# All fp32r products stream their columns backwards, and the weight ring moves by 256 bytes

## The chip, the cores and the metric

The kernel runs on one core of one Trainium2 chip. The metric is the device time of one launch in microseconds (us). The tensor engine (TensorE, PE in the profile) multiplies; VectorE (DVE), ScalarE (ACT) and GpSimd (POOL) do the rest; SyncE (SP) issues most of the DMAs. SBUF is the on-chip memory that TensorE reads; PSUM is the one that it writes.

## The reference

One decoder layer on an input of 256 tokens by 4096 channels, all in float32. Reduced to what costs time:

```
xn = rmsnorm(x);  p = xn @ w_in                 # 4096 -> 5200 columns, and the gates' 4096 -> 256
o_a, o_b, o_c, o_d = four causal attentions(p)  # 4 to 6 heads of 128 each
m = sum over branches: sigmoid(z @ gate_up[i]) * (o_i @ w_branch[i])   # -> 4096
h = x + m @ w_out                               # 4096 -> 4096
hn = rmsnorm(h);  q = hn @ peer_wq              # 4096 -> 1024, top-k expert keys
act = gelu(hn @ peer_u.T)                       # 4096 -> 4096
out = h + (sparse weights * act) @ peer_v       # 4096 -> 4096
```

Nearly all of the work is in the dense products with w_in, gate_up, w_branch, w_out, peer_wq, peer_u and peer_v.

## The kernel before

**Split products.** Each float32 operand is split into a high part in the type fp32r and a low part (value minus high part), also in fp32r. One float32 product becomes three fp32r matmuls: high times high, high times low, low times high. The activations are the stationary operand, a tile of 128 by 128 (512 bytes in each partition), kept transposed in `xt_hi`/`xt_lo` and, by stage, `x2_*`, `x3_*`, `ot_*`, `zt_*`, `s_*`. The weights are the moving operand, 512 columns wide (2048 bytes in each partition). They come from HBM in chunks of 256 rows by 512 columns.

**The weight ring.** A chunk s passes through slot s % 4 of three buffers: `w_raw` (SP's DMA), `w_hi` (ACT, line 1199: a rounding copy), `w_lo` (DVE, line 1608: raw minus high). TensorE waits for `hi_ready`, issues the eight matmuls that need `w_hi`, waits for `lo_ready`, issues the four that need `w_lo`, and raises `chunk_used`, which frees the slot. The three buffers stand one behind the other from `RG0`; every slot is 4096 bytes.

**Twelve matmuls to a chunk.** `products` (lines 668 to 684) runs two halves of 128 rows (j) times two halves of the tokens (h), three times over, into two PSUM banks. Each matmul has a stationary tile of its own, so each record of a matmul has a record of a weight load (LDWEIGHTS, engine PEld) beside it. The first group of columns (`first_products`, line 686) is 336 wide, all the others 512. `branch_products` (line 712) is the same by token half. In the products with w_out and peer_v, `fast_products` (line 1052) uses sums of operands, `t_*` moving against `xt_*` and `s_*` stationary, to save some matmuls; `plain_products` and `last_products` (line 1112, 256 columns wide) are the rest.

**Other users of TensorE.** Between chunks `between(s)` inserts the small work at fixed slots: transposes (line 780), attention scores and values in plain float32 (lines 854, 889 and others), one-hot products in bf16 (line 966). These are not fp32r.

**Where the tiles stand.** SBUF is laid out by hand: `XT0` is the base, `RG0` the ring 64 KB further, `MG0` a work area behind the ring, `CN0` constants behind that, and `PJ0` the projections behind the constants, where `x2_*`, `ot_*`, `zt_*` and `t_*` live too. The constants ahead of PJ0 take 512 + 128 + 128 + 1280 = 2048 bytes. So before the change XT0, RG0, MG0 and PJ0 all have the same address modulo 512: every moving and every stationary tile of an fp32r product begins at the same place modulo 512, but for the second half of a chunk in the 336-wide group, which begins 1344 bytes (320 modulo 512) further.

Of the kernel before, what the change touches and what calls it, by code (L numbers as in the profile page):

```python
# [28 lines left out]
P = 128  # L29
S = 256  # L30
NT = S // P
# [202 lines left out]
def build(nc, io):  # L234

    base = (nc.sbuf_base + 31) // 32 * 32
    XT0 = base
    RG0 = XT0 + 64 * KB
    MG0 = RG0 + 12 * RING * KB
    CN0 = MG0 + 32 * KB  # L240

# [31 lines left out]
    ident = const("ident", [P, P])  # L273
    g_mix = const("g_mix", [P, KT])
    g_ffn = const("g_ffn", [P, KT])
    small = const("small", [P, 320])
    PJ0 = cursor[0]

    proj = const("proj", [P, NT, NCOL])
# [213 lines left out]
    def pair_bank(pair, i):  # L493

        return group_number(pair, i) % 2
# [72 lines left out]
    with nc.Block() as block:  # L568
# [96 lines left out]

        @block.tensor
        def _(pe):
            def products(parity, chunk, slot, lhs, k0, width, first, last):

                wh = [w_hi[:, slot, j * width:(j + 1) * width] for j in range(2)]  # L670
                wl = [w_lo[:, slot, j * width:(j + 1) * width] for j in range(2)]
                o = [acc[:, parity, h, 0:width] for h in range(NT)]
                pe.wait_ge(hi_ready, chunk + 1)
                for j in range(2):
                    for h in range(NT):
                        pe.matmul(o[h], lhs(k0 + j, h)[0], wh[j], start=first and j == 0, stop=False)  # L676
                for j in range(2):
                    for h in range(NT):
                        pe.matmul(o[h], lhs(k0 + j, h)[1], wh[j], start=False, stop=False)  # L679
                pe.wait_ge(lo_ready, chunk + 1)  # L680
                for j in range(2):
                    for h in range(NT):
                        mm = pe.matmul(o[h], lhs(k0 + j, h)[0], wl[j], start=False, stop=last and j == 1)  # L683
                mm.then_inc(chunk_used, 1)

            def first_products(chunk, slot, width):

                pe.wait_ge(hi_ready, chunk + 1)
                wh = [w_hi[:, slot, j * width:(j + 1) * width] for j in range(2)]
                wl = [w_lo[:, slot, j * width:(j + 1) * width] for j in range(2)]  # L690
                k0, o = 2 * chunk, [acc[:, 0, h, 0:width] for h in range(NT)]
                for j in range(2):
                    pe.wait_ge(xt_hi_done, k0 + j + 1)
                    for h in range(NT):
                        pe.matmul(o[h], xt(k0 + j, h)[0], wh[j], start=k0 + j == 0, stop=False)
                for j in range(2):
                    pe.wait_ge(xt_lo_done, k0 + j + 1)
                    for h in range(NT):
                        pe.matmul(o[h], xt(k0 + j, h)[1], wh[j], start=False, stop=False)
                pe.wait_ge(lo_ready, chunk + 1)  # L700
                for j in range(2):
                    for h in range(NT):
                        mm = pe.matmul(o[h], xt(k0 + j, h)[0], wl[j], start=False, stop=k0 + j == KT - 1)
                mm.then_inc(chunk_used, 1)
# [7 lines left out]
            def branch_products(chunk, slot, lhs, k0, first, last, before):  # L712

                pe.wait_ge(hi_ready, chunk + 1)
                wh = [w_hi[:, slot, j * 512:(j + 1) * 512] for j in range(2)]
                wl = [w_lo[:, slot, j * 512:(j + 1) * 512] for j in range(2)]
                for h in range(NT):
                    if first and h == 0 and before:
                        pe.wait_ge(term_half, before)
                    elif first:  # L720
                        bank(0, (GN_MIX + 1) // 2 + before)
                    o = acc[:, 0, h, :]
                    for j in range(2):
                        pe.matmul(o, lhs(k0 + j, h)[0], wh[j], start=first and j == 0, stop=False)  # L724
                    for j in range(2):
# [314 lines left out]
                return pe.matmul(o, pair[0], moving[1][j], start=False, stop=stop)  # L1040

            def ring(slot):
                return [[w[:, slot, j * 512:(j + 1) * 512] for j in range(2)] for w in (w_hi, w_lo)]

            def wait_block(pair, i, h):

# [5 lines left out]
            def fast_products(pair, kp):  # L1052
# [2 lines left out]
                first, last, opens = kp == pair.fast[0], kp == pair.fast[-1], kp == 0  # L1055
                wa, wb = ring(a % RING), ring((a + 1) % RING)
                s_tile = s_tiles(pair, kp)
                t = [[w[:, i // 2, i % 2, :] for i in range(4)] for w in t_tiles[pair in OUT_PAIRS][1:]]
                c11, c21, c12 = (acc[:, pair_bank(pair, i), h, :] for i, h in ((0, 0), (0, 1), (1, 0)))

                def from_t():
                    for d in range(2):
                        pe.wait_ge(t_hi_done, 2 * n + d + 1)
                        pe.wait_ge(t_lo_done, 2 * n + d + 1)
                        if d == 0:
                            thrice(side[:, 1, :], s_tile[0], t, 0, first, last)
                            thrice(side[:, 3, :], s_tile[2], t, 1, first, last)
                        else:
                            thrice(side[:, 2, :], s_tile[1], t, 2, first, last)

                of_ring = ((side[:, 0, :], xt(2 * kp, 0), wa, 0, first), (c11, xt(2 * kp + 1, 0), wa, 1, opens),
                           (c12, s_tile[3], wb, 1, opens))

                def by_hi(i):
# [37 lines left out]
            def last_products(slot, kp):  # L1112

                for side_n in range(2):
                    cols = slice(side_n * 256, side_n * 256 + 256)
                    o = side[:, side_n, 0:256]
                    for j in range(2):
                        wh, wl = (w[:, slot, j * 512:(j + 1) * 512][:, cols] for w in (w_hi, w_lo))
                        xh, xl = xt(2 * kp + j, 1)
                        pe.matmul(o, xh, wh, start=j == 0, stop=False)  # L1120
                        pe.matmul(o, xl, wh, start=False, stop=False)
# [5 lines left out]
            def plain_products(pair, kp, i):  # L1127
# [14 lines left out]
                for h in range(NT):  # L1142
                    if kp == 1 and h == 1:
                        wait_block(pair, 1, 1)
                    if s == CH_END - 1 and h == 1:
                        pe.wait_ge(pure_free, pair.order + 1)
                        mm = last_products(slot, kp)
                        continue
                    o = acc[:, pair_bank(pair, i), h, :]
                    for p in range(2):  # L1150
                        for j in range(2):
                            pe.matmul(o, xt(2 * kp + j, h)[p], w[0][j],  # L1152
# [1414 lines left out]
```

## Time and profile before

| | |
|---|---|
| times of three runs | 1908.01, 1908.49, 1910.51 us; median 1908.49 us |
| the profiled execution: span from its first to its last instruction | 1906.1 us |
| median minus that span | 2.4 us |
| PE busy, matmuls | 1900.6 us, 8941 |
| PEld busy, weight loads | 1567.2 us, 8941 |
| DVE busy | 1463.9 us (77%) |
| ACT busy | 984.9 us (52%) |
| DMA | 412.69 MB, mean 217 GB/s |
| TensorE clock granted | full speed in all 40 slices |

The profile gives of the profiled execution its span; no second time of its own is recorded for it. Matmuls are pipelined and their ends are modelled: the busy time of a matmul (389 ns for 512 columns) is longer than the distance to the next one's start, so consecutive records overlap. What a matmul costs in a stream is the distance from one start to the next. It is read from the timeline, where a row "start, length, line, xN" stands for N matmuls in a row: the difference of two rows' starts divided by N.

### The profile page before, as it was taken

Reading aid. Unit: us, or ns where it says so; the run is one execution under the profiler, and the core shown is the slowest. Engines: PE = TensorE matmul, PEld = TensorE weight load, DVE = VectorE, ACT = ScalarE, POOL = GpSimd, SP = SyncE. Lnnn points to the kernel's source line nnn. Section 1 sums busy time; section 2 is a strip of 40 time slices with the busy share of each in tenths; the row PEclk is TensorE's granted clock in tenths of the full one; section 3 lists DMA queues with packets and bytes.
Section 4 is the critical chain, followed back from the end, with each engine's and each line's share of the span. In section 5 each row is a group of like instructions: output and inputs, shape, how many; then the busy total and the mean of one; then the engine's idle time right before and its main releaser. Section 6 shows DMA issues by size and latency. Waiting matters only on the chain.

```text
span 1906.1 us, 25847 instructions
## 1 busy us (share of the span) xinstructions
PE 1900.6 (100%) x8941; PEld 1567.2 (82%) x8941; DVE 1463.9 (77%) x2139; ACT 984.9 (52%) x1214; POOL 36.2 (2%) x49
## 2 busy tenths in 40 slices
PE   9999999999999999999999999999999999999999
PEld 8888888888888888888888888888887788888887
DVE  7578775584556889889765555899988878999897
ACT  6653644445456655546454464444444455555553
POOL 0010010000000000000000000000000000000000
PEclk9999999999999999999999999999999999999999
DMA  9976666655655668877887776767766668666664
GB/s 326 344 226 166 172 174 199 176 156 157 191 177 178 185 190 288 278 226 238 254 256 234 216 226 218 232 208 221 219 201 198 197 208 290 223 213 218 210 219 155
DMA packets 198832, 412.69 MB, mean 217 GB/s; under 512 B 45792, under 2 KB 124256, under 8 KB 198080
## 3 DMA queue, kind: packets, MB, share of 16 engines
q1 hardware_dynamic: 174048, 369.35, 63.0%
q10 hardware_dynamic: 20976, 25.19, 3.9%
q0 software_dynamic: 3696, 16.65, 2.4%
q8 instruction: 71, 1.16, 0.2%
q14 instruction: 41, 0.34, 0.1%
HBM read 390.15 MB, written 20.97 MB: 216 GB/s over the span
## 4 chain that ended last, share of the span: by engine, by line
PE 97%; DVE 2%; DMA 0%; issue 0%; ACT 0%; SPq 0%; DVEq 0%; ACTq 0%
PE acc L676 25%; PE acc L679 25%; PE acc L683 25%; PE acc L724 3%; PE acc L726 3%; PE acc L730 3%; PE side L1039 1%; PE side L1038 1%; PE acc L1152 1%; PE side L1040 1%; PE acc L1079 1%; PE acc L1085 1%; PE side L854 1%; PE acc L1080 1%; PE side L966 1%; DVE w_lo L1608 1%
## 5 line engine op out<-in xcount | busy, mean ns | idle before, releaser
L1608 DVE TENSOR_TENSOR w_lo<-w_raw,w_hi 128x1024 fp32r<-128x1024 f32 (+1 forms) x649 | 785.6, 1214 | 389.7 <-ACT w_hi L1199 384.9
L1199 ACT ACTIVATE w_hi<-w_raw 128x1024 fp32r<-128x1024 f32 (+1 forms) x649 | 681.1, 1052 | 701.2 <-PE acc L683 577.5
L676 PE MATMUL acc<-w_hi,xt_hi 128*128 128x512 f32 x1348 | 365.7, 393 | 0.0
L679 PE MATMUL acc<-w_hi,xt_lo 128*128 128x512 f32 x1348 | 360.8, 390 | 0.0
L683 PE MATMUL acc<-w_lo,xt_hi 128*128 128x512 f32 x1348 | 360.6, 389 | 0.0
L679 PEld LDWEIGHTS acc<-w_hi,xt_lo 128*128 128x128 f32 x1348 | 253.1, 188 | 53.1
L683 PEld LDWEIGHTS acc<-w_lo,xt_hi 128*128 128x128 f32 x1348 | 253.1, 188 | 52.9
L676 PEld LDWEIGHTS acc<-w_hi,xt_hi 128*128 128x128 f32 x1348 | 250.2, 188 | 51.5 <-issue 1.8
L676 PE MATMUL acc<-w_hi,x_hi 128*128 128x512 f32 x640 | 175.1, 396 | 0.0
L679 PE MATMUL acc<-w_hi,x_lo 128*128 128x512 f32 x640 | 171.5, 390 | 0.0
L683 PE MATMUL acc<-w_lo,x_hi 128*128 128x512 f32 x640 | 171.4, 390 | 0.0
L679 PEld LDWEIGHTS acc<-w_hi,x_lo 128*128 128x128 f32 x640 | 120.2, 188 | 25.6
L683 PEld LDWEIGHTS acc<-w_lo,x_hi 128*128 128x128 f32 x640 | 120.2, 188 | 25.6
L676 PEld LDWEIGHTS acc<-w_hi,x_hi 128*128 128x128 f32 x640 | 117.3, 188 | 22.1
L1552 ACT ACTIVATE t_hi<-t_raw 128x1024 fp32r<-128x1024 f32 x46 | 47.4, 1057 | 22.5 <-PE acc L1040 19.2
L2277 DVE TENSOR_TENSOR t_lo<-t_raw,t_hi 128x1024 fp32r<-128x1024 f32 x46 | 54.2, 1220 | 0.0
L1341 ACT ACTIVATE gate<-acc 128x512 f32<-128x512 f32 x64 | 34.8, 596 | 37.3 <-PE acc L683 35.7
L676 PE MATMUL acc<-w_hi,zt_hi 128*128 128x512 f32 x128 | 34.5, 392 | 0.0
L679 PE MATMUL acc<-w_hi,zt_lo 128*128 128x512 f32 x128 | 34.3, 390 | 0.0
L683 PE MATMUL acc<-w_lo,zt_hi 128*128 128x512 f32 x128 | 34.3, 390 | 0.0
L1853 DVE TENSOR_TENSOR gate<-acc,gate 128x512 f32<-128x512 f32 x48 | 30.8, 683 | 0.0
L1283 ACT ACTIVATE probs<-probs,small 128x128 f32<-128x128 f32 (+2 forms) x44 | 18.3, 417 | 22.0 <-DVE small L1766 21.9
(376 smaller groups left out, 2061.5 us busy)
## 6 DMA issues: line engine op xcount, KB each, us to landing
w_raw<-in_stream SPq DMA_DIRECT2D x504, 512.0 KB, 4.2
w_raw<-in_w_in SPq DMA_DIRECT2D x16, 496.0 KB, 4.1
w_raw<-in_w_in SPq DMA_DIRECT2D x16, 480.0 KB, 3.9
w_raw<-in_w_in SPq DMA_DIRECT2D x16, 464.0 KB, 3.8
w_raw<-in_w_in SPq DMA_DIRECT2D x16, 448.0 KB, 3.9
w_raw<-in_w_in SPq DMA_DIRECT2D x16, 432.0 KB, 3.9
w_raw<-in_w_in SPq DMA_DIRECT2D x16, 416.0 KB, 4.0
w_raw<-in_w_in SPq DMA_DIRECT2D x16, 400.0 KB, 3.8
```

The source lines that it names most:

```text
L676: pe.matmul(o[h], lhs(k0 + j, h)[0], wh[j], start=first and j == 0, stop=False)
L679: pe.matmul(o[h], lhs(k0 + j, h)[1], wh[j], start=False, stop=False)
L683: mm = pe.matmul(o[h], lhs(k0 + j, h)[0], wl[j], start=False, stop=last and j == 1)
L724: pe.matmul(o, lhs(k0 + j, h)[0], wh[j], start=first and j == 0, stop=False)
L726: pe.matmul(o, lhs(k0 + j, h)[1], wh[j], start=False, stop=False)
L730: mm = pe.matmul(o, lhs(k0 + j, h)[0], wl[j], start=False, stop=last and j == 1)
L1199: nc.scalar.activation(w_hi[:, slot, 0:width], w_raw[:, slot, 0:width], ACT.Copy).then_inc(hi_ready, 1)
L1341: e = nc.scalar.activation(gate[:, n % 2, h, :], acc[:, 1, h, :], ACT.Sigmoid)
L1552: nc.scalar.activation(flat(hi_tile[:, d]), flat(raw[:, d]), ACT.Copy).then_inc(t_hi_done, 1)
L1608: nc.vector.tensor_tensor(w_lo[:, slot, 0:width], w_raw[:, slot, 0:width], w_hi[:, slot, 0:width].bitcast(F32), ALU.subtract).then_inc(lo_ ...
L1853: nc.vector.tensor_tensor(dst, acc[:, 0, h, :], gate[:, n % 2, h, :], ALU.mult)\
L2277: nc.vector.tensor_tensor(flat(lo_tile[:, d]), flat(raw[:, d]), flat(hi_tile[:, d]).bitcast(F32), ALU.subtract).then_inc(t_lo_done, 1)
```

## The change

All matmuls on fp32r operands get their moving operand and their output with the columns in descending order (`[:, ::-1]` on both, through a helper `back`), so that the same products land in the same places, last column first. The stationary operands, the plain float32 and the bf16 matmuls keep their order. `RG0` moves up by 256 bytes, and with it `MG0` and `CN0`; the constant `small` shrinks from 320 to 256 columns (206 are used), which puts `PJ0` back where it was. So the ring and the tiles at MG0 (`s_*`, `wmat`, parts of the `out_*` tiles) stand 256 bytes off the others modulo 512, and the stationary tiles `xt_*`, `x2_*`, `x3_*`, `ot_*`, `zt_*` stay. The number and the order of the instructions, the waits and the DMAs are as before.

```diff
--- before.py
+++ after.py
@@ -235,7 +235,7 @@
 
     base = (nc.sbuf_base + 31) // 32 * 32
     XT0 = base
-    RG0 = XT0 + 64 * KB
+    RG0 = XT0 + 64 * KB + 256
     MG0 = RG0 + 12 * RING * KB
     CN0 = MG0 + 32 * KB
 
@@ -273,7 +273,7 @@
     ident = const("ident", [P, P])
     g_mix = const("g_mix", [P, KT])
     g_ffn = const("g_ffn", [P, KT])
-    small = const("small", [P, 320])
+    small = const("small", [P, 256])
     PJ0 = cursor[0]
 
     proj = const("proj", [P, NT, NCOL])
@@ -665,11 +665,15 @@
 
         @block.tensor
         def _(pe):
+            def back(row):
+
+                return row[:, ::-1]
+
             def products(parity, chunk, slot, lhs, k0, width, first, last):
 
-                wh = [w_hi[:, slot, j * width:(j + 1) * width] for j in range(2)]
-                wl = [w_lo[:, slot, j * width:(j + 1) * width] for j in range(2)]
-                o = [acc[:, parity, h, 0:width] for h in range(NT)]
+                wh = [back(w_hi[:, slot, j * width:(j + 1) * width]) for j in range(2)]
+                wl = [back(w_lo[:, slot, j * width:(j + 1) * width]) for j in range(2)]
+                o = [back(acc[:, parity, h, 0:width]) for h in range(NT)]
                 pe.wait_ge(hi_ready, chunk + 1)
                 for j in range(2):
                     for h in range(NT):
@@ -686,9 +690,9 @@
             def first_products(chunk, slot, width):
 
                 pe.wait_ge(hi_ready, chunk + 1)
-                wh = [w_hi[:, slot, j * width:(j + 1) * width] for j in range(2)]
-                wl = [w_lo[:, slot, j * width:(j + 1) * width] for j in range(2)]
-                k0, o = 2 * chunk, [acc[:, 0, h, 0:width] for h in range(NT)]
+                wh = [back(w_hi[:, slot, j * width:(j + 1) * width]) for j in range(2)]
+                wl = [back(w_lo[:, slot, j * width:(j + 1) * width]) for j in range(2)]
+                k0, o = 2 * chunk, [back(acc[:, 0, h, 0:width]) for h in range(NT)]
                 for j in range(2):
                     pe.wait_ge(xt_hi_done, k0 + j + 1)
                     for h in range(NT):
@@ -712,14 +716,14 @@
             def branch_products(chunk, slot, lhs, k0, first, last, before):
 
                 pe.wait_ge(hi_ready, chunk + 1)
-                wh = [w_hi[:, slot, j * 512:(j + 1) * 512] for j in range(2)]
-                wl = [w_lo[:, slot, j * 512:(j + 1) * 512] for j in range(2)]
+                wh = [back(w_hi[:, slot, j * 512:(j + 1) * 512]) for j in range(2)]
+                wl = [back(w_lo[:, slot, j * 512:(j + 1) * 512]) for j in range(2)]
                 for h in range(NT):
                     if first and h == 0 and before:
                         pe.wait_ge(term_half, before)
                     elif first:
                         bank(0, (GN_MIX + 1) // 2 + before)
-                    o = acc[:, 0, h, :]
+                    o = back(acc[:, 0, h, :])
                     for j in range(2):
                         pe.matmul(o, lhs(k0 + j, h)[0], wh[j], start=first and j == 0, stop=False)
                     for j in range(2):
@@ -1040,7 +1044,7 @@
                 return pe.matmul(o, pair[0], moving[1][j], start=False, stop=stop)
 
             def ring(slot):
-                return [[w[:, slot, j * 512:(j + 1) * 512] for j in range(2)] for w in (w_hi, w_lo)]
+                return [[back(w[:, slot, j * 512:(j + 1) * 512]) for j in range(2)] for w in (w_hi, w_lo)]
 
             def wait_block(pair, i, h):
 
@@ -1055,20 +1059,21 @@
                 first, last, opens = kp == pair.fast[0], kp == pair.fast[-1], kp == 0
                 wa, wb = ring(a % RING), ring((a + 1) % RING)
                 s_tile = s_tiles(pair, kp)
-                t = [[w[:, i // 2, i % 2, :] for i in range(4)] for w in t_tiles[pair in OUT_PAIRS][1:]]
-                c11, c21, c12 = (acc[:, pair_bank(pair, i), h, :] for i, h in ((0, 0), (0, 1), (1, 0)))
+                t = [[back(w[:, i // 2, i % 2, :]) for i in range(4)] for w in t_tiles[pair in OUT_PAIRS][1:]]
+                p1, p5, p6, p7 = (back(side[:, i, :]) for i in range(4))
+                c11, c21, c12 = (back(acc[:, pair_bank(pair, i), h, :]) for i, h in ((0, 0), (0, 1), (1, 0)))
 
                 def from_t():
                     for d in range(2):
                         pe.wait_ge(t_hi_done, 2 * n + d + 1)
                         pe.wait_ge(t_lo_done, 2 * n + d + 1)
                         if d == 0:
-                            thrice(side[:, 1, :], s_tile[0], t, 0, first, last)
-                            thrice(side[:, 3, :], s_tile[2], t, 1, first, last)
+                            thrice(p5, s_tile[0], t, 0, first, last)
+                            thrice(p7, s_tile[2], t, 1, first, last)
                         else:
-                            thrice(side[:, 2, :], s_tile[1], t, 2, first, last)
-
-                of_ring = ((side[:, 0, :], xt(2 * kp, 0), wa, 0, first), (c11, xt(2 * kp + 1, 0), wa, 1, opens),
+                            thrice(p6, s_tile[1], t, 2, first, last)
+
+                of_ring = ((p1, xt(2 * kp, 0), wa, 0, first), (c11, xt(2 * kp + 1, 0), wa, 1, opens),
                            (c12, s_tile[3], wb, 1, opens))
 
                 def by_hi(i):
@@ -1113,9 +1118,9 @@
 
                 for side_n in range(2):
                     cols = slice(side_n * 256, side_n * 256 + 256)
-                    o = side[:, side_n, 0:256]
+                    o = back(side[:, side_n, 0:256])
                     for j in range(2):
-                        wh, wl = (w[:, slot, j * 512:(j + 1) * 512][:, cols] for w in (w_hi, w_lo))
+                        wh, wl = (back(w[:, slot, j * 512:(j + 1) * 512][:, cols]) for w in (w_hi, w_lo))
                         xh, xl = xt(2 * kp + j, 1)
                         pe.matmul(o, xh, wh, start=j == 0, stop=False)
                         pe.matmul(o, xl, wh, start=False, stop=False)
@@ -1146,7 +1151,7 @@
                         pe.wait_ge(pure_free, pair.order + 1)
                         mm = last_products(slot, kp)
                         continue
-                    o = acc[:, pair_bank(pair, i), h, :]
+                    o = back(acc[:, pair_bank(pair, i), h, :])
                     for p in range(2):
                         for j in range(2):
                             pe.matmul(o, xt(2 * kp + j, h)[p], w[0][j],
```

## Rows read from the trace of the kernel before

**Rows 1.** The page: busy time, share of the span, instructions; granted clock in 40 slices.

```profile
PE 1900.6 (100%) x8941; PEld 1567.2 (82%) x8941; DVE 1463.9 (77%) x2139; ACT 984.9 (52%) x1214; POOL 36.2 (2%) x49
...
PEclk9999999999999999999999999999999999999999
```

**Rows 2.** The chain that ended last, share of the span by engine.

```profile
PE 97%; DVE 2%; DMA 0%; issue 0%; ACT 0%; SPq 0%; DVEq 0%; ACTq 0%
```

**Rows 3.** Waits of PE: line, waited for, us in total, times, longest.

```profile
PE acc L1079 <- DVE h_rows L2329: 1.3, 3, 0.4
PE side L710 <- DVE warm L2355: 1.3, 1, 1.3
PE acc L695 <- ACT w_hi L1199: 0.2, 1, 0.2
```

**Rows 4.** Costliest groups of matmuls: line, tiles, count | busy us, mean ns | idle.

```profile
L676 PE MATMUL acc<-w_hi,xt_hi 128*128 128x512 f32 x1348 | 365.7, 393 | 0.0
...
L676 PE MATMUL acc<-w_hi,x_hi 128*128 128x512 f32 x640 | 175.1, 396 | 0.0
...
L676 PE MATMUL acc<-w_hi,zt_hi 128*128 128x512 f32 x128 | 34.5, 392 | 0.0
```

**Rows 5.** Timeline of PE, 560 to 566 us (start, length, line, tiles, count): fp32r, 512 wide.

```profile
562.30 1.07 PE L676 MATMUL acc<-w_hi,zt_hi 128*128 128x512 f32 x4
...
565.02 0.61 PE L724 MATMUL acc<-w_hi,ot_b_hi 128*128 128x512 f32 x2
```

**Rows 6.** Timeline of PE, 15 to 20 us: fp32r, 336 wide.

```profile
16.02 0.78 PE L695 MATMUL acc<-w_hi,xt_hi 128*128 128x336 f32 x4
...
18.47 0.78 PE L699 MATMUL acc<-w_hi,xt_lo 128*128 128x336 f32 x4
```

**Rows 7.** Timeline of PE, 1900 us to the end: fp32r, 256 wide.

```profile
1901.96 0.28 PE L1121 MATMUL side<-w_hi,xt_lo 128*128 128x256 f32 x1
...
1903.16 0.28 PE L1122 MATMUL side<-w_lo,xt_hi 128*128 128x256 f32 x1
```

**Rows 8.** Timeline of PE, 398 to 404 us: plain float32, 512 wide.

```profile
400.31 1.88 PE L889 MATMUL side<-probs_t,proj 128*128 128x512 f32 x4
402.02 1.89 PE L854 MATMUL side<-feat_c 128*128 128x256 f32 x8
```

**Rows 9.** Timeline of PE, 1440 to 1444 us: bf16, 96 wide.

```profile
1440.85 0.52 PE L966 MATMUL side<-hot_q,hot_c 128*128 128x96 bf16 x8
1441.19 1.17 PE L676 MATMUL acc<-w_hi,x_hi 128*128 128x512 f32 x4
```

**Rows 10.** Matmuls that read w_lo: duration ns least/median/most, first and last start.

```profile
L683 PE MATMUL acc<-w_lo,xt_hi x1348: 388/389/399, 38.1 to 1894.8; 128*128 128x512 f32 x193
```

**Rows 11.** Timeline of PE, 303.8 to 312 us, between two batches of transposes.

```profile
303.88 1.08 PE L679 MATMUL acc<-w_hi,xt_lo 128*128 128x512 f32 x4
304.80 1.08 PE L683 MATMUL acc<-w_lo,xt_hi 128*128 128x512 f32 x4
```

**Rows 12.** Stretches of 20 us: PE, PEld, DVE, ACT, POOL busy (count), clock, DMA share, GB/s.

```profile
20.00:40.00 20.00, 20.00 (x125) 19.33 (x124) 16.90 (x27) 15.84 (x26) 0.00 (x0) 1.00 0.98 329
...
60.00:80.00 20.00, 20.00 (x90) 16.57 (x89) 8.58 (x7) 12.29 (x15) 1.09 (x3) 1.00 0.97 336
...
740.00:760.00 20.00, 20.00 (x90) 16.58 (x89) 19.93 (x24) 13.35 (x19) 0.00 (x0) 1.00 0.92 303
760.00:780.00 20.00, 20.00 (x90) 16.58 (x89) 19.90 (x23) 10.73 (x14) 0.54 (x1) 1.00 0.96 313
...
880.00:900.00 20.00, 20.00 (x89) 16.55 (x89) 19.86 (x27) 12.36 (x15) 0.00 (x0) 1.00 0.60 198
...
1260.00:1280.00 20.00, 20.00 (x90) 16.55 (x89) 19.49 (x35) 7.91 (x8) 0.00 (x0) 1.00 0.79 236
```

## What was predicted

> **What bounds the kernel now.** I read the busy shares and the chain first. PE is busy for 100% of the span and holds 97% of the chain that ended last [rows 1, 2]; its waits on other engines sum to 2.8 us [rows 3], and the granted clock is full, 2.4 GHz, in all 40 slices [rows 1]. So the time is the number of matmuls times the distance between their starts, and an edit that touches neither count nor order can act only through that distance. Busy time does not show it, since records overlap; the timeline does.
>
> In the steady stream of 512 columns, twelve starts take 565.02 - 562.30 = 2.72 us, 226.7 ns each [rows 5]. 512 columns at one per clock of 2.4 GHz are 213.3 ns, so 13.3 ns are lost per matmul. At 336 columns, 16 starts take 2.45 us, 153.1 ns, against 140.0: 13.1 ns [rows 6]. At 256 columns, ten take 1.20 us, 120.0 against 106.7: 13.3 ns [rows 7]. The loss does not grow with the columns; it belongs to something that occurs once per matmul, and each matmul has one weight load of 128 columns.
>
> Is it the load as such? Plain float32 matmuls also have one load of 128 float32 columns each. Four of 512 columns take 1.71 us, 427.5 ns each [rows 8], which is 512 columns at two clocks each (426.7) plus 1 ns. Bf16 products of 96 columns, each with a load too, take 0.34 us for eight, 42.5 ns against 40.0 [rows 9]: 2.5 ns. So changing the weights costs at most about 2.5 ns when the moving stream reads float32 at half the rate or reads half the bytes. The other 10.8 ns appear only where the moving operand is read at 4 bytes per clock while the load reads its 512 bytes. That looks like two reads of the same memory getting into each other's way. A second sign is that the distance is not quite rigid: the duration of one fp32r matmul goes from 388 to 399 ns around a median of 389 [rows 10], and behind a batch of transposes, which shifts load against stream, four matmuls take 0.92 us, 230 ns each, instead of 226.7 [rows 11]. Same instructions, same addresses, other relative timing, other price.
>
> **The change part by part.**
>
> *Reversed columns and shifted ring, together.* They alter the addresses that the two reads touch at the same moment. In the kernel before, all stationary and moving tiles begin at the same place modulo 512 (a stationary tile is 512 bytes). The one exception is the second half of each 336-wide chunk, 320 bytes further, and the mean over both halves is 13.1 ns there against 13.3 elsewhere [rows 5, 6]: in the present direction the starting place does not matter. That is what two streams running against each other would give: they cross as often wherever they start. Two streams in the same direction keep more of their distance, and there the start does matter. If the weight load reads its tile from the last column, reversing the moving stream makes the two run alike, and 256 of 512 bytes is the farthest apart that they can be put. Both edits fit this reading.
>
> The bounds of the effect per matmul: removed down to the bf16 row, 226.7 to 215.8, is -10.8 ns; removed wholly is -13.3 ns; worse by as much as the longest record, 399 - 389, is +10 ns; a stable worst like rows 11 is +3.3 ns. Nothing of before runs backwards, so a descending read or write may also be slow as such: the nearest row is two clocks per column, 427.5 ns [rows 8], +200 ns. I take -10.8 ns, because all rows in which the two reads are not both at full rate agree on 2.5 ns or less.
>
> The count: three passes of line 676's groups are 3 x (1348 + 640 + 128) = 6348 [rows 4]. The other fp32r lines (695 to 703, 724 to 730, 1038 to 1040, 1079 to 1085, 1120 to 1122, 1152, 1158) bring 1725 more, from 224 each on lines 724, 726 and 730 down to 4 each on lines 1120 to 1122; 8073 of 8941. All stand on PE's chain, end to end. 8073 x 10.8 ns = 87.2 us.
>
> *What comes up when PE is faster.* PE's pace rises by 226.7 / 215.8 = 1.05; 20 us of its work would take 19.04 us. DVE is busy for more than that in eleven stretches of 20 us: 19.93, 19.90 and 19.86 in the worst three, 19.49 in the next [rows 12]. Its excess over 19.04 summed over the eleven is 4.7 us. The ring of four chunks, some 10 us of PE's work, smooths within that but doesn't remove it. DMA is at 0.97 to 1.05 of its share from 20 to 100 us, with the input's rows and the weights together (the first and third of these stretches are in [rows 12]), so those 80 us cannot shrink: 80 x 0.048 = 3.8 us. Given back: 8.5 us.
>
> *The rest.* `MG0` and `CN0` move by 256 bytes, `small` becomes narrower and `PJ0` stays. ACT, DVE and DMA get other addresses and no other instruction. I cost that at nothing: 1 ns per DVE or ACT instruction, either way, would be 2139 and 1214 ns of engines that stand idle for 442 and 921 us [rows 1]; in the stretches where DVE is full it would be some 0.1 us. The tiles at MG0 (`s_*` against the ring, and some of the `out_*` tiles), and `t_*` against `xt_*`, end up in phase rather than 256 bytes apart. They are products on lines 1038 to 1040 and 1079 to 1085, at most 651 of 8073; if all of these kept their 10.8 ns, 7 us would be lost. Part of them are 256 apart, and I leave it to the range.
>
> **Sum.** 1906.1 - 87.2 + 8.5 = 1827.4 us of span. The median of the runs lies 2.4 us above the profiled span, so 1830 us.
>
> **Two rules of the Trainium skill.** The trace shows a loss of 13.3 ns that comes with the load [rows 5 to 7]. The Trainium skill's page "TensorE: Matmul & The Clock Gate", section "Step-by-step: what each phase is for", says that the moving operand and the weight load have two independent read ports and that loading the next weights takes no read bandwidth from the running matmul. By that rule there is nothing here to win, and the time stays at 1908; by the rows, the load costs something in fp32r and hardly anything in float32. The Trainium skill's page "PSUM — Partial Sum Buffer", section "Specifications (TRN2)", says that PSUM works in lines of 8 bytes and that any non-contiguous pattern slows matmuls significantly; no row of before shows how the chip treats a descending one. It bears on rival 4.
>
> **The rivals.**
> *1. Partly removed.* The reversed streams still meet in places, or the lines that end up in phase pay. Half of the 10.8 ns gives 8073 x 5.4 = 43.6 us less and no bound of DVE worth counting: 1865 us. For it: the price moved by only a few ns with timing [rows 10, 11].
> *2. Nothing changes.* The load takes its 13.3 ns, 32 clocks of 2.4 GHz, whatever addresses meet: it is the same at three widths, and the starting place was indifferent at 336 columns [rows 6]. 1908 us. Against it: rows 10 and 11, where the price varied.
> *3. The streams lock badly: slower.* Running alike, they can stay in collision for the whole load where they formerly only crossed. Every load whose tile meets the moving stream in step then pays, from the first chunk on. At +3.3 ns [rows 11] it is 26.6 us, 1935 us; at +10 ns [rows 10] it is 80.7 us, 1989 us. It decides as soon as the stream's distance is above 227.5 ns. Nothing in the trace fixes the order in which a load reads its tile, so the sign of my argument is not secured.
> *4. Backward is slow in itself.* Two clocks per column add 200 ns to each of 8073: 1615 us, about 3520 us. For it: no row, since nothing of before runs backwards. Against it: no column is read or written more often than before.
>
> **How the numbers follow.** Removed to about 2.5 ns: 0.42, 1812 to 1845 us by itself. Partly removed: 0.20. Nothing: 0.15. Badly locked: 0.18. Backward slow: 0.05. Faster by over 0.2% (which is about what a measurement of this kernel can tell from no change) is 0.62, within it 0.15, slower 0.23. The range 1812 to 1920 holds the first three and the mildest of the fourth.
>
> **What would show it.** The same stretch of the timeline, twelve starts of 512 columns: 2.59 us if right, 2.66 if half, 2.72 if nothing, 2.76 or more if locked, 5.1 if slow. The last products, 256 wide, would stand 109 ns apart instead of 120. The plain float32 and bf16 rows stay. PE's waits would no longer be near zero: some 4 us on DVE's `w_lo` around 740 to 780 us and 1260 to 1360 us of the old time, and some 4 us on ACT's `w_hi` behind DMA in the first 100. If the distance falls but differs between lines 676 and 1038 to 1040, the phase decides and not the direction. The argument is wrong if the distance does not move at all, or if it falls although no wait or order changed and the price at 256 columns stays 13.3 ns.

## The result, and the profile after: slower by 2.5%

The changed kernel takes 1956.24 us (median of 4, 1955.77 to 1956.39), the kernel before beside it 1908.94 us (1908.01 to 1910.51). The ratio is 1.0248, with a 95% interval of 1.0235 to 1.026. Forecast were 1830 us and a range of 1812 to 1920, so sign and range were wrong.

The page of the changed kernel shows the same instructions, the same clock, and PE busy from end to end. The columns are those of [rows 1, 2]:

```profile
span 1954.4 us, 25847 instructions
...
PE 1949.9 (100%) x8941; PEld 1569.6 (80%) x8941; DVE 1464.2 (75%) x2139; ACT 984.7 (50%) x1214; POOL 36.6 (2%) x49
...
PEclk9999999999999999999999999999999999999999
...
PE 99%; DMA 0%; SPq 0%; ACT 0%; DVE 0%; issue 0%
```

DVE, ACT and POOL are busy as long as before [rows 1], to within half a microsecond. PE's busy time grew by 49.3 us (1949.9 - 1900.6) and the span by 48.3. PE's waits stay near nothing (line, waited for, us in total, times, longest), so the time went into the matmuls themselves:

```profile
PE side L714 <- DVE warm L2360: 1.3, 1, 1.3
PE acc L699 <- ACT w_hi L1204: 0.4, 1, 0.4
```

The costliest groups (busy us, mean ns of one), which answer to [rows 4], have grown by 7 to 8 ns per matmul:

```profile
L680 PE MATMUL acc<-w_hi,xt_hi 128*128 128x512 f32 x1348 | 374.4, 401 | 0.0
...
L680 PE MATMUL acc<-w_hi,x_hi 128*128 128x512 f32 x640 | 178.9, 403 | 0.0
...
L680 PE MATMUL acc<-w_hi,zt_hi 128*128 128x512 f32 x128 | 35.4, 399 | 0.0
```

The timeline of PE in the changed kernel (start, length, line, tiles, count) has the stretch of [rows 5] at 575 us:

```profile
575.39 1.10 PE L680 MATMUL acc<-w_hi,zt_hi 128*128 128x512 f32 x4
...
578.19 0.63 PE L728 MATMUL acc<-w_hi,ot_b_hi 128*128 128x512 f32 x2
```

Twelve starts take 578.19 - 575.39 = 2.80 us, 233.3 ns each, where they took 226.7: 6.7 ns more. These rows give starts to 0.01 us, so a stretch of twelve fixes the distance to 0.8 ns, one of four only to 2.5 ns. At 336 columns [rows 6] sixteen take 19.12 - 16.65 = 2.47 us, 154.4 ns, 1.3 more. At 256 [rows 7] ten take 1951.43 - 1950.24 = 1.19 us, 119 ns: no more than before.

```profile
16.65 0.78 PE L699 MATMUL acc<-w_hi,xt_hi 128*128 128x336 f32 x4
...
19.12 0.78 PE L703 MATMUL acc<-w_hi,xt_lo 128*128 128x336 f32 x4
...
1950.24 0.28 PE L1126 MATMUL side<-w_hi,xt_lo 128*128 128x256 f32 x1
...
1951.43 0.28 PE L1127 MATMUL side<-w_lo,xt_hi 128*128 128x256 f32 x1
```

The matmuls that read `w_lo` had durations of 388/389/399 ns [rows 10] and now, least, median and most:

```profile
L687 PE MATMUL acc<-w_lo,xt_hi x1348: 397/397/398, 39.0 to 1942.9; 128*128 128x512 f32 x193
```

The stream is slower and at the same time rigid. That also accounts for the sum. The trace has 7794 distances between two neighbouring matmuls of 512 columns; their mean went from 228.8 to 234.8 ns, and this makes 46.9 us of the 48.3. The gain per start is 6.0 ns and not 6.7, since the kernel before already lost some pace behind inserts: 717 of its distances lie between 228 and 300 ns, and in the changed kernel only 40 lie between 235 and 300. One such place before is [rows 11], where line 679 takes 229.5 ns per start by the trace; the same place in the changed kernel keeps its usual pace, 0.93 us for four:

```profile
305.21 1.10 PE L683 MATMUL acc<-w_hi,xt_lo 128*128 128x512 f32 x4
306.14 1.10 PE L687 MATMUL acc<-w_lo,xt_hi 128*128 128x512 f32 x4
```

### The profile page after: what moved, and what is told of

Same layout as the page of the kernel before. It is cut to its first block, busy times and chain, and to the rows that moved or that the text cites. A ratio compares the mean times of both kernels' runs of the same rounds, so it can differ in the third digit from the quotient of the medians.

```text
span 1954.4 us, 25847 instructions
## 1 busy us (share of the span) xinstructions
PE 1949.9 (100%) x8941; PEld 1569.6 (80%) x8941; DVE 1464.2 (75%) x2139; ACT 984.7 (50%) x1214; POOL 36.6 (2%) x49
## 3 DMA queue, kind: packets, MB, share of 16 engines
q0 software_dynamic: 3696, 16.65, 2.4%
## 4 chain that ended last, share of the span: by engine, by line
PE 99%; DMA 0%; SPq 0%; ACT 0%; DVE 0%; issue 0%
PE acc L680 25%; PE acc L683 25%; PE acc L687 25%; PE acc L728 3%; PE acc L730 3%; PE acc L734 3%; PE acc L1157 2%; PE side L1042 1%; PE side L1043 1%; PE side L1044 1%; PE acc L1163 1%; PE acc L1084 1%; PE acc L1085 1%; PE acc L1090 1%; PE side L858 1%; PE side L970 1%
## 5 line engine op out<-in xcount | busy, mean ns | idle before, releaser
L680 PE MATMUL acc<-w_hi,xt_hi 128*128 128x512 f32 x1348 | 374.4, 401 | 0.0
L687 PE MATMUL acc<-w_lo,xt_hi 128*128 128x512 f32 x1348 | 369.8, 397 | 0.0
L683 PE MATMUL acc<-w_hi,xt_lo 128*128 128x512 f32 x1348 | 369.8, 397 | 0.0
L687 PE MATMUL acc<-w_lo,x_hi 128*128 128x512 f32 x640 | 175.6, 397 | 0.0
L683 PE MATMUL acc<-w_hi,x_lo 128*128 128x512 f32 x640 | 175.6, 397 | 0.0
L2268 DVE TENSOR_TENSOR t_raw<-w_raw 128x1024 f32<-128x1024 f32 x23 | 28.1, 1220 | 2.2 <-DMA w_raw<-in_stream 1.9
```

## The experiments

The kernel before has a median between 1908.2 and 1908.7 us in each set of runs. "Backward" is from the last column to the first.

**Which edit, and which operand.** Four kernels each do one part. The first is the changed kernel without the 256 bytes; the second has only the 256 bytes; the third and fourth are the changed kernel with the ring at its old place, and reverse only what is read, or only what is written. One line of each edit is shown for them.

```diff
 e1_backward_only, against the changed kernel
-    RG0 = XT0 + 64 * KB + 256
+    RG0 = XT0 + 64 * KB
 e2_shift_only, against the kernel before
-    RG0 = XT0 + 64 * KB
+    RG0 = XT0 + 64 * KB + 256
 e3_read_back: back() stands around w_hi, w_lo and t_* alone
-                o = [back(acc[:, parity, h, 0:width]) for h in range(NT)]
+                o = [(acc[:, parity, h, 0:width]) for h in range(NT)]
 e4_write_back: back() stands around acc and side alone
-                wh = [back(w_hi[:, slot, j * width:(j + 1) * width]) for j in range(2)]
+                wh = [(w_hi[:, slot, j * width:(j + 1) * width]) for j in range(2)]
```

In the third and fourth the columns land mirrored, so they compute something else with the same work.

> All fp32r products backwards, ring where it was. Locking theory (rival 3: two streams running alike meet or miss by their starting places): without the 256 bytes the distance must differ clearly from the changed kernel's 233.3 ns, towards 216 or towards 240 and more, 1825 or 2010 us. Direction theory (backward columns cost whatever the starting places are): 233.3 ns and 1956 us as in the changed kernel.

> Columns forward, ring 256 bytes further modulo 512. Locking theory: in the old direction the starting place was indifferent at 336 columns, so 226.7 ns and 1908 us. Direction theory: the same, 1908 us. If the shift carried the loss, 233 ns and 1956 us.

> Ring where it was; only the moving operand is read backwards, the output is written forwards, so the columns land mirrored in their bank (the result is not the reference's). If the loss lies in the read: 233.3 ns, 1956 us. If it lies in the write of PSUM: 226.7 ns, 1908 us. If each has its share: between.

> Ring where it was; the moving operand is read forwards, only the output is written backwards (columns land mirrored, the result is not the reference's). If the loss lies in the read: 226.7 ns, 1908 us. If in the write: 233.3 ns, 1956 us.

Measured: e1 1956.09 us, ratio 1.0248 (1.0231 to 1.0265); e2 1908.88, 0.9999 (0.999 to 1.0009); e3 1956.10, 1.0247 (1.023 to 1.0264); e4 1908.78, 1.000 (0.9991 to 1.001). The durations of one and the same group, first in e1, then e2, e3 and e4:

```profile
L683 PE MATMUL acc<-w_hi,xt_lo x1348: 397/397/398, 37.4 to 1941.3; 128*128 128x512 f32 x193
```

```profile
L679 PE MATMUL acc<-w_hi,xt_lo x1348: 387/389/398, 37.1 to 1894.8; 128*128 128x512 f32 x193
```

```profile
L683 PE MATMUL acc<-w_hi,xt_lo x1348: 397/397/398, 37.8 to 1941.7; 128*128 128x512 f32 x193
```

```profile
L683 PE MATMUL acc<-w_hi,xt_lo x1348: 387/389/398, 36.9 to 1893.6; 128*128 128x512 f32 x193
```

So reading the moving operand backward is the whole loss. Writing the output backward costs nothing that shows, and 256 bytes change nothing in either direction.

**How fine must the order be?** Columns are taken in groups of 4 (16 bytes), with the ring at its old place: the groups backward and their inside forward (e7), or the groups forward and their inside backward (e8).

```diff
 e7_fours_back
-                return row[:, ::-1]
+                b, n = 4, row.shape[1] // 4
+                return row.rearrange("p (n b) -> p n b", b=b)[:, ::-1, :]
 e8_in_fours_back: the same with
+                return row.rearrange("p (n b) -> p n b", b=b)[:, :, ::-1]
```

> Ring where it was; every fp32r row is read and written in groups of four columns (16 bytes), the groups from last to first and the four of a group forwards. If the run of the address through the row is what costs (the moving stream then goes the way the loads may go): 233.3 ns between starts, 1956 us. If the order inside four columns costs: 226.7 ns, 1908 us.

> The counterpart: groups of four columns from first to last, the four of a group backwards. Run of the address: 226.7 ns, 1908 us. Order inside four: 233.3 ns, 1956 us. If both come below, then the two-level pattern itself matters.

Measured: e7 1956.08 us, 1.0248 (1.023 to 1.0265); e8 1908.56, 1.000 (0.999 to 1.0009). Durations in e7, then in e8:

```profile
L684 PE MATMUL acc<-w_hi,xt_lo x1348: 397/397/398, 37.7 to 1941.6; 128*128 128x512 f32 x193
```

```profile
L684 PE MATMUL acc<-w_hi,xt_lo x1348: 387/389/398, 36.8 to 1894.4; 128*128 128x512 f32 x193
```

The order inside 16 bytes is free, read and written; the order of the pieces of 16 bytes is what costs.

**Is it a collision with the weight load?** If it is, a load of half the columns should meet the stream for a shorter time. The second and third pass of `products` load and compute only 64 of the 128 stationary columns and leave out half of their output rows, in the forward kernel (e9) and the backward one (e10, ring at its old place). The first pass keeps whole loads.

```diff
-                        pe.matmul(o[h], lhs(k0 + j, h)[1], wh[j], start=False, stop=False)
+                        pe.matmul(o[h][0:64], lhs(k0 + j, h)[1][:, 0:64], wh[j], start=False, stop=False)
...
+                n = P if last else 64
...
-                        mm = pe.matmul(o[h], lhs(k0 + j, h)[0], wl[j], start=False, stop=last and j == 1)
+                        mm = pe.matmul(o[h][0:n], lhs(k0 + j, h)[0][:, 0:n], wl[j], start=False, stop=last and j == 1)
```

> Columns forwards. The high-by-low and low-by-high products of the common chunk routine (lines 679 and 684, all but the last of a group) load 64 stationary columns instead of 128 and leave half of their rows out (the result is not the reference's). If the 13.3 ns belong to the load and grow with its columns: 220.0 ns on these, some 4000 x 6.7 = 27 us less, 1881 us. If they are a fixed price of a change of weights: 226.7 ns, 1908 us.

> The same half loads with all columns backwards. If the whole 20.0 ns of the backward stream is collision with the load: half of it goes, 223.3 ns on these, 4000 x 10 = 40 us less than 1956, 1916 us. If the backward stream costs 6.7 ns by itself and the load 13.3: 226.7 ns on these, 1929 us. If neither shrinks with the load: 1956 us.

Measured: e9 1926.0 us, 1.0091 (1.0074 to 1.0108), slower than whole loads; e10 1956.34, 1.0249 (1.0232 to 1.0266), as without the edit. The loads did become shorter. These are the weight loads of e10 (busy us, mean ns | idle us), and the durations of its matmuls:

```profile
L680 PEld LDWEIGHTS acc<-w_hi,xt_hi 128*128 128x128 f32 x1348 | 250.5, 188 | 72.5 <-issue 1.8
...
L683 PEld LDWEIGHTS acc<-w_hi,xt_lo 128*64 128x64 f32 x1348 | 182.0, 135 | 114.7
```

```profile
L683 PE MATMUL acc<-w_hi,xt_lo x1348: 397/397/398, 37.9 to 1941.8; 128*64 128x512 f32 x193
```

135 instead of 188 ns of loading take nothing off the backward price. A price that grows with the length of the load is ruled out by this; a collision of fixed length is not. In the forward kernel the even pace was lost instead. The durations in e9 begin and end near those of the kernel before (388/389/399 [rows 10]), with a larger median:

```profile
L684 PE MATMUL acc<-w_lo,xt_hi x1348: 387/392/401, 38.0 to 1912.4; 128*64 128x512 f32 x182, 128*128 128x512 f32 x11
```

**Does the place matter?** In e12 (forward) and e11 (backward) the ring's slots stand at several offsets to the stationary tiles; `MG0` moves by 320 bytes as well. The expectation of e11 takes 320 bytes off for all tiles behind the ring. That holds for those at `MG0`; those from `PJ0` on, `x2_*`, `ot_*` and `zt_*` among them, stand 320 - 256 = 64 bytes further, since `small` is narrower by 256 bytes. In e18, e19 and e20 (forward) the whole ring stands 32, 64 or 128 bytes further; `MG0` moves by 256 bytes in all three.

```diff
 e11_phases_back, e12_phases
-    w_hi = at("w_hi", [P, RING, 1024], F32R, RG0 + 4 * RING * KB)
-    w_lo = at("w_lo", [P, RING, 1024], F32R, RG0 + 8 * RING * KB)
+    w_hi = at("w_hi", [P, RING, 1028], F32R, RG0 + 4 * RING * KB)
+    w_lo = at("w_lo", [P, RING, 1040], F32R, RG0 + 8 * RING * KB + 64)
 e18_ring_32; with 64 and 192 in e19_ring_64, with 128 and 128 in e20_ring_128
-    RG0 = XT0 + 64 * KB
-    MG0 = RG0 + 12 * RING * KB
+    RG0 = XT0 + 64 * KB + 32
+    MG0 = RG0 + 12 * RING * KB + 224
```

> Columns backwards; the slots of w_hi start 0, 16, 32 and 48 bytes off the stationary tiles modulo 64, those of w_lo 64, 128, 192 and 256 bytes modulo 512 (all less 320 bytes for the tiles that live behind the ring). If two streams running alike meet or miss by their starting places, the distance must differ from slot to slot and by line (672 to 679 against 683). If the starting place plays no part: 233.3 ns in every slot, 1956 us.

> The same layout with the columns forwards. Starting place of no part: 226.7 ns in every slot, 1908 us. If some starting place is better than that of the kernel before, its slot shows under 226 ns and the time falls below 1906 us.

> Columns forwards; the whole ring starts 32 bytes off the stationary tiles (modulo 64 and 512), the tiles behind it 256. If the slower pace of e12 (some 231 ns) came from the starting place: other than 226.7 ns, and 1930 to 1945 us. If it came only from starting places that change from slot to slot: 226.7 ns, 1908 us.

> As e18 with 64 bytes. If only the place inside 64 bytes counts: 226.7 ns, 1908 us. If the place inside 512 bytes counts: other than 226.7 ns.

> Columns forwards, the whole ring 128 bytes off the stationary tiles. 0 and 256 bytes gave 226.7 ns, 32 gave 233.5, 64 gave 228.9. If the place repeats every 128 bytes: 226.7 ns, 1908 us. If it repeats every 256 and 128 is the far point: another distance; under 226 ns it would beat the kernel before, over 229 ns the time is above 1925 us.

Measured: e11 1959.65 us, 1.0266 (1.0249 to 1.0283); e12 1944.33, 1.0186 (1.0169 to 1.0203); e18 1953.69, 1.0237 (1.022 to 1.0254); e19 1924.68, 1.0085 (1.0069 to 1.0102); e20 1949.22, 1.0214 (1.0197 to 1.0231). Forward, an offset alone costs up to 45 us. Steady stretches of the timeline in e18, e19 and e20:

```profile
574.26 1.09 PE L676 MATMUL acc<-w_hi,zt_hi 128*128 128x512 f32 x4
...
577.06 0.63 PE L724 MATMUL acc<-w_hi,ot_b_hi 128*128 128x512 f32 x2
```

```profile
566.25 1.08 PE L676 MATMUL acc<-w_hi,zt_hi 128*128 128x512 f32 x4
...
568.99 0.62 PE L724 MATMUL acc<-w_hi,ot_b_hi 128*128 128x512 f32 x2
```

```profile
573.94 1.10 PE L676 MATMUL acc<-w_hi,zt_hi 128*128 128x512 f32 x4
...
576.73 0.63 PE L724 MATMUL acc<-w_hi,ot_b_hi 128*128 128x512 f32 x2
```

They are 2.80 / 12 = 233.3 ns, 2.74 / 12 = 228.3 and 2.79 / 12 = 232.5, against 226.7 at 0 and 256 bytes. At 32 bytes the forward stream thus has the pace of the backward one. The place decides in the forward direction, and the kernel before stands at the best place tried.

Backward, the offsets of e11 add 3.6 us to e1 in sum, but they do act. Two passes of e11 read the same slot of `w_lo`. The first has stationary tiles of `x2_hi`, which stand 64 bytes further, the second those of `x3_hi`, which did not move:

```profile
1357.26 1.12 PE L687 MATMUL acc<-w_lo,x_hi 128*128 128x512 f32 x4
1358.22 1.11 PE L680 MATMUL acc<-w_hi,x_hi 128*128 128x512 f32 x4
...
1368.54 1.10 PE L687 MATMUL acc<-w_lo,x_hi 128*128 128x512 f32 x4
1369.47 1.10 PE L680 MATMUL acc<-w_hi,x_hi 128*128 128x512 f32 x4
```

The first takes 0.96 us, 240 ns per start, the second 0.93 us, 232.5. The moving addresses are equal, so the place of the stationary tile counts too, and not only that of the moving one. Over all groups of this stage the two passes average 238.7 and 233.1 ns.

**Only fp32r?** e13 reads the plain float32 operands (128 and 256 wide) and the bf16 ones (96 wide) backward and leaves fp32r forward.

```diff
+                def matmul(self, o, still, moving, **kw):
+                    plain = moving.dtype != F32R and len(moving.shape) == 2 and len(o.shape) == 2
+                    if plain and moving.shape[1] in (96, 128, 256):
+                        moving, o = moving[:, ::-1], o[:, ::-1]
+                    return self.pe.matmul(o, still, moving, **kw)
```

> fp32r forwards as in the kernel before; the plain float32 products of 128 and 256 columns (line 854 and others) and the bf16 products of 96 columns (line 966) read and write backwards. If a backward read is dear as such: 256 columns of float32 stand over 215.7 ns apart and 96 of bf16 over 42.5 ns. If only fp32r at 4 bytes per clock pays: both stay. The time stays at 1908 us either way, since these are some 300 short matmuls.

Measured: 1908.46 us, 1.0001 (0.999 to 1.0011). The bf16 group's mean duration is 207 ns here and 208 in the kernel before, and the distance between the float32 matmuls of 256 columns has a median of 216 ns in both. So these two kinds pay nothing at 96 to 256 columns. That doesn't show that only fp32r pays: the run left the float32 matmuls of 512 columns (line 889) forward, and at 256 columns fp32r pays nothing either, as e16 and e17 below show. The type isn't separated from the width.

```profile
L680 PE MATMUL side<-hot_q,hot_c 128*128 128x96 bf16 x256 | 16.5, 207 | 0.0
```

**Does each matmul pay for itself?** e14 reads backward in one pass of three (line 679) only. e15 keeps the columns forward inside blocks and reverses the blocks: 256 columns on line 676's pass, 64 on 679's, 16 on 683's.

```diff
 e14_one_pass_back
-                        pe.matmul(o[h], lhs(k0 + j, h)[1], wh[j], start=False, stop=False)
+                        pe.matmul(o[h][:, ::-1], lhs(k0 + j, h)[1], wh[j][:, ::-1], start=False, stop=False)
 e15_blocks: with 256, 64 and 16 in the three passes
+            def blocks(row, b):
+
+                return row.rearrange("p (n b) -> p n b", b=b)[:, ::-1, :] if row.shape[1] == 512 else row
```

> Only the high-by-low products of the common chunk routine (line 679, 2116 of 8073) run backwards, the rest forwards. If each backward matmul pays for itself: 233.3 ns on line 679, 226.7 on the others, 1908 + 2116 x 6.7 ns = 1923 us. If the even pace of the forward stream is lost by any disturbance, the forward lines rise too, to 229 to 231 ns, and the time to 1930 us or more.

> Blocks from last to first with the columns of a block forwards: blocks of 256 on line 679's first pass partner (high by high), of 64 on high by low, of 16 on low by high. If the steady run of the address through the whole row decides, blocks of 256 and 64 cost little (226 to 229 ns) and 16 is nearer to 233.3. If the first read (the end of the row) decides, all three show 233.3 ns.

Measured: e14 1930.69 us, 1.0119 (1.0102 to 1.0135); e15 1933.3, 1.0131 (1.0114 to 1.0148). In e14, the backward pass has its full price, and the forward pass behind it pays too. The steady cycle of twelve:

```profile
324.29 1.07 PE L676 MATMUL acc<-w_hi,xt_hi 128*128 128x512 f32 x4
325.20 1.10 PE L679 MATMUL acc<-w_hi,xt_lo 128*128 128x512 f32 x4
326.13 1.09 PE L683 MATMUL acc<-w_lo,xt_hi 128*128 128x512 f32 x4
327.06 1.07 PE L676 MATMUL acc<-w_hi,xt_hi 128*128 128x512 f32 x4
```

Four starts fix a distance to 2.5 ns only. The mean of the 297 cycles without an insert in this trace is 226.7 ns on line 676, 234.2 on 679 and 230.9 on 683. Line 679 has 2116 of the 8073 matmuls, 26%, and the run pays 22.4 us, 47% of the whole loss. In e15, the same cycles show 230.4 ns (blocks of 256), 229.6 (64) and 233.3 (16); the line before in the order disturbs the line after, as e14 shows, so they can't be read as the price of each block size. I leave the order among them open.

**What does it grow with?** In e16 (backward) and e17 (forward) the second pass is cut into two of 256 columns (shown) and the third into 384 + 128; the ring stands at its old place in both.

```diff
-                        pe.matmul(o[h], lhs(k0 + j, h)[1], wh[j], start=False, stop=False)
+                        for c in parts(width, 256):
+                            pe.matmul(o[h][:, c], lhs(k0 + j, h)[1], wh[j][:, c], start=False, stop=False)
```

> All backwards; the high-by-low products are cut into two of 256 columns, the low-by-high ones into 384 and 128. The changed kernel shows +11.6 ns over the bare columns at 256, +14.9 at 336, +20 at 512. If the extra of backward reads grows with the columns: 118 ns at 256, 177 at 384, and at 128 columns 62 ns or the load's own length, 109 ns. If it is a fixed price, 256 shows 126 to 127 ns. Time: 4232 extra matmuls, some 2010 to 2200 us.

> The cuts of e16 with everything forwards. Forward reads pay 13.3 ns over the bare columns at 256, 336 and 512. If that is a fixed price of a matmul: 120 ns at 256 columns, so each cut pair is slower than with backward reads (118.3 ns each), by some 4 ns a pair. If forward reads, too, pay by columns: below 118 ns at 256.

Measured: 2078.24 us backward and 2058.0 forward. Both are above the kernel before, since there are more matmuls; the difference between them is 20.2 us. Timelines of e16, then e17, with eight matmuls of 256 columns each:

```profile
603.80 1.11 PE L688 MATMUL acc<-w_hi,zt_lo 128*128 128x256 f32 x8
604.75 1.26 PE L693 MATMUL acc<-w_lo,zt_hi 128*128 128x384 f32 x8
```

```profile
590.20 1.10 PE L684 MATMUL acc<-w_hi,zt_lo 128*128 128x256 f32 x8
591.13 1.26 PE L689 MATMUL acc<-w_lo,zt_hi 128*128 128x384 f32 x8
```

These single stretches give 0.95 / 8 = 118.8 ns backward and 0.93 / 8 = 116.3 forward, each good to 1.3 ns. They don't stand for the rest: over all 3703 distances between two matmuls of 256 columns of this pass the mean is 118.5 ns backward and 118.4 forward, and the mean durations over 2696 of them are 282 and 281 ns. A pair of 384 + 128 costs 1.6 ns more backward. So no backward price shows at 256 columns, and it is there at 512: the matmuls that stayed whole, at most 8073 - 2 x 2116 = 3841, would account with 6.0 ns each for 23 us, the whole difference of 20.2. In the changed kernel the time over the bare columns is 119 - 106.7 = 12 ns at 256, 14.4 at 336 and 20.0 at 512. Forward it is 13.3 at all three widths [rows 5 to 7] and 11.7 in the cut stream of e17.

## Why the prediction was wrong

*What bounds the kernel* held. PE's chain is 99% of the span, no wait came or went, and the time is the distance between starts times their number. The count of 8073 held too: 8073 x 6.0 ns = 48.4 us is the loss.

*"Two reads of the same memory getting into each other's way"* held in kind. e12 and e18 to e20 alter nothing but addresses, and the distance goes from 226.7 to 228.3, 232.5 and 233.3 ns. A shift of the ring alone could act through the moving read's own place; e11 shows that at equal moving addresses the stationary tile's place counts as well (238.7 against 233.1 ns). This also measures the Trainium skill's rule of two independent read ports (page "TensorE: Matmul & The Clock Gate", section "Step-by-step: what each phase is for"). By that rule, the place of one read against the other would not alter the time; the runs disagree by up to 45 us. It gave no price for reading backward either.

**The step that failed** is this one: "If the weight load reads its tile from the last column, reversing the moving stream makes the two run alike, and 256 of 512 bytes is the farthest apart that they can be put." It turned the loss of 13.3 ns in the present direction into a gain of 10.8 in the other. Reversed, each start costs 6.7 ns more (e3), at an offset of 0 as at 256 bytes (e1, after). I had shown that something costs 10.8 ns, not that the other direction is without it. No run shows the -10.8 ns; in their place stand +6.7 ns in the steady stream and +6.0 over all starts.

*"In the present direction the starting place does not matter"* also failed. The 336-wide chunks gave one other offset, 320 bytes. If the pattern repeats every 256 bytes, as 0 and 256 being equal suggests but doesn't show, that is 64, which is the mildest of the offsets measured (1924.68 us), and only half of those matmuls had it. One sample was read as a rule. The kernel before owes its 226.7 ns to equal places; a shift of 32 bytes costs nearly as much as the reversal, 45 against 47 us.

*The -10.8 ns and the bounds.* The upper bound, +10 ns from the longest record, held the measured +6.7. The +3.3 ns of [rows 11] came from four starts, and so is good to 2.5 ns; the trace has 229.5 ns there, +2.8. The likeliest value was chosen by "all rows in which the two reads are not both at full rate agree", which says what the price would be without fp32r, not what reversal does.

*What comes up when PE is faster*: the 8.5 us of DVE and DMA never arose, since PE became slower; they are untested. *The rest*, MG0 and CN0 at nothing, held: e2 has the same moves and is at 0.9999.

*The rivals.* Rival 3, "the streams lock badly: slower", had 0.18 and is the one that came as to sign, time (1935 to 1989 us) and sign in the timeline (2.76 us or more; 2.80). Its mechanism is only half borne out. The stream is in fact locked, 397/397/398. But a collision "for the whole load" should shrink with half the load, and e10 shows no change. The place matters backward at the finer offsets of e11, yet in no slot does a pass average less than 232 ns; they lie around the 233.3 of e1. Rival 2, nothing, is refuted; rival 4 is refuted as to its price, two clocks per column, though not as to its kind, a backward read that is slow in itself. The argument against it, that no column is touched more often, did not protect: e7 and e8 show that the order of 16-byte pieces costs by itself. The rule of the page "PSUM — Partial Sum Buffer" of the Trainium skill (section "Specifications (TRN2)"), that non-contiguous patterns slow matmuls, does not reach to a descending write: e4 stands at 1.000.

*The signs.* "If the distance falls but differs between lines 676 and 1038 to 1040, the phase decides and not the direction": it rose, and stands at 233.3 ns on both (lines 680 and 1042 to 1044 in the changed kernel). This sign could not tell, since 0 and 256 bytes are alike forward as well (e2). Plain float32 and bf16, left forward, stayed, as forecast.

**Still open.** What makes a backward read cost 6.7 ns at 512 columns and nothing that shows at 256. It could be the general price of two reads out of step, which equal places escape in the forward direction alone: e18's 233.3 ns is the same pace. It could also be a price of the backward stream by itself. No run tells this apart, since none streams backward without a load of weights beside it. Whether float32 or bf16 of 512 columns pays was not tried, nor were stationary tiles read in the other order; of the offsets of a whole ring only 0, 32, 64, 128 and 256 bytes were. No kernel beat the one before.

## What to carry to other kernels

Where PE bounds a kernel of fp32r matmuls, read the distance between starts and compare it with the columns; then place ring and stationary tiles 0 or 256 bytes apart modulo 512, the two places that were best here, and read forward; measure any other shift, since 32 bytes cost 2.4%. An argument from "this costs time" to "the reverse saves it" needs a row of the reverse. Where none exists, the sign is open, and one kernel that reverses only the read settles it before anything else is built on it.

## What was not expected of the hardware

- A moving fp32r operand of 512 columns read backward: 233.3 ns per start against 226.7; at 256 columns 118.5 against 118.4 (e16, e17). Float32 and bf16 of 96 to 256 columns pay none (e13).
- The order of four columns inside 16 bytes is free (e8: 1908.56 us), as is a descending write (e4: 1908.78 us).
- Offsets between moving and stationary tiles cost 16 us at 64 bytes, 41 at 128 and 45 at 32, none at 256. With the moving addresses equal, 64 bytes in the stationary tile's place make 238.7 ns out of 233.1 (e11, backward).
- Half as many stationary columns shorten a load from 188 to 135 ns and make the forward kernel 18 us slower, at the same number of moving columns.
- Line 679 alone backward, 26% of the matmuls, takes 47% of the full price; the forward pass behind it is slowed as well, to 230.9 ns (e14).
